# First norm's load order, split last products, and two rests moved from Pool to DVE in a two-layer hybrid trunk

## The reference

```python
def rmsnorm(x, w):
    y = xf * lax.rsqrt(jnp.mean(xf * xf, axis=-1, keepdims=True) + EPS) * w

def attn_pool_mixer(u, w_in, sinks, pool_w, pool_scale, w_out):
    proj = u @ w_in
    ...                                   # a: attention, m: pooled means times pool_w
    return jnp.concatenate([a, m], axis=-1) @ w_out

def swiglu(h, w_gate, w_up, w_down):
    return (jax.nn.silu(h @ w_gate) * (h @ w_up)) @ w_down

    for layer in range(DEPTH):
        h = rmsnorm(x, mix_norm_w[layer])
        x = x + (attn_pool_mixer if layer % 2 == 0 else ssd_mixer)(h, ...)
        x = x + swiglu(rmsnorm(x, ffn_norm_w[layer]), w_gate[layer], w_up[layer], w_down[layer])
    return rmsnorm(x, final_norm_w)
```

## Time and profile before

| | us |
|---|---|
| median of 3 runs | 2375.91 |
| range of the runs | 2374.59 to 2376.46 |
| the profiled execution | 2377.45 |
| its span in the trace | 2375.7 |
| PE busy / DVE / ACT / Pool busy | 2310.3 / 1269.2 / 1067.4 / 1207.6 |

### The profile page before, as it was taken

The page is one execution under the profiler, slowest core; times in us unless marked ns, Lnnn a source line. Parts: engine busy times, 40 slices in busy tenths (PEclk is TensorE's granted clock), DMA queues, the critical chain, the costliest instruction groups (busy, mean ns, idle before and its releaser), DMA issues.

```text
span 2375.7 us, 29380 instructions
## 1 busy us (share of the span) xinstructions
PE 2310.3 (97%) x10850; PEld 1882.3 (79%) x10850; DVE 1269.2 (53%) x1662; ACT 1067.4 (45%) x1888; POOL 1207.6 (51%) x852
## 2 busy tenths in 40 slices
PE   7999999999999999999999999999999999999997
PEld 5867778888888888777877887887878888887886
DVE  6447563333336787467257347438762433335776
ACT  4036553333333446375266248238543333333444
POOL 3223287777774654224224214314287777774653
PEclk9999999999999999999999999999999999999999
DMA  5100223323238753121221212122213323227744
GB/s 154 49 27 19 102 65 118 115 85 115 85 111 287 243 151 94 56 81 54 63 71 54 67 41 89 39 59 80 91 61 132 116 84 116 85 98 275 254 148 142
DMA packets 166786, 247.89 MB, mean 104 GB/s; under 512 B 18416, under 2 KB 111484, under 8 KB 164092
## 3 DMA queue, kind: packets, MB, share of 16 engines
q1 hardware_dynamic: 161020, 230.06, 29.7%
q10 hardware_dynamic: 5632, 15.99, 1.7%
HBM read 192.93 MB, written 53.08 MB: 104 GB/s over the span
## 4 chain that ended last, share of the span: by engine, by line
PE 85%; DVE 6%; issue 2%; ACT 2%; POOL 2%; DMA 1%; SPq 0%; DVEq 0%; ACTq 0%; POOLq 0%
PE ps L1383 27%; PE ps L1385 26%; PE ps L1384 26%; PE ps L1854 1%; POOL p_lo L752 1%; PE ps L1406 1%; DVE acc L2463 1%; PE ps L1841 1%; DVE mdec L2502 1%; DMA d_val<-in_w_down 1%; PE ps L1548 1%; DVE yx L2531 1%; POOL p_val L776 1%; PE ps L1846 1%; PE ps L1569 1%
## 5 line engine op out<-in xcount | busy, mean ns | idle before, releaser
L727 POOL TENSOR_TENSOR w_lo<-w_raw,w_hi 128x1024 fp32r<-128x1024 f32 x74 | 181.2, 2453 | 337.2 <-ACT w_hi L898 327.0
L829 POOL TENSOR_TENSOR s_lo<-s_val,s_hi 128x512 fp32r<-128x512 f32 x154 | 233.8, 1520 | 207.9 <-ACT s_hi L1199 207.7
L1383 PE MATMUL ps<-xn_hi,w_hi 128*128 128x512 f32 x800 | 319.5, 399 | 5.0 <-DVE xn_lo L1976 2.5
L2134 DVE TENSOR_TENSOR xres<-ps,xres 128x512 f32<-128x512 f32 x132 | 90.8, 689 | 433.6 <-PE ps L1385 422.5
L1384 PE MATMUL ps<-xn_lo,w_hi 128*128 128x512 f32 x800 | 314.1, 393 | 0.0
L1385 PE MATMUL ps<-xn_hi,w_lo 128*128 128x512 f32 x800 | 313.7, 392 | 0.0
L1383 PE MATMUL ps<-xn_hi,p_hi 128*128 128x512 f32 x704 | 274.5, 390 | 0.8 <-POOL p_lo L752 0.6
L1385 PE MATMUL ps<-xn_hi,p_lo 128*128 128x512 f32 x704 | 273.9, 389 | 0.0
L1384 PE MATMUL ps<-xn_lo,p_hi 128*128 128x512 f32 x704 | 273.9, 389 | 0.0
L752 POOL TENSOR_TENSOR p_lo<-p_val,p_hi 128x512 fp32r<-128x512 f32 x176 | 237.3, 1357 | 36.5 <-ACT p_hi L1018 36.5
L1018 ACT ACTIVATE p_hi<-p_val 128x512 fp32r<-128x512 f32 x176 | 111.2, 632 | 306.8 <-POOL p_val L776 306.8
(11 more groups left out here) (269 smaller groups left out, 5160.0 us busy)
## 6 DMA issues: line engine op xcount, KB each, us to landing
s_val<-hidden SPq DMA_DIRECT2D x154, 256.0 KB, 2.8
hidden<-xres SPq DMA_DIRECT2D x20, 1792.0 KB, 6.6
wv_g<-in_w_gate SPq DMA_DIRECT2D x22, 1024.0 KB, 5.3
wv_u<-in_w_up SPq DMA_DIRECT2D x22, 1024.0 KB, 5.2
w_raw<-in_ssd_w_in SPq DMA_DIRECT2D x40, 512.0 KB, 3.9
d_val<-in_w_down SPq DMA_DIRECT2D x70, 256.0 KB, 4.0
rows_v<-in_w_down SPq DMA_DIRECT2D x64, 256.0 KB, 3.6
mdec<-decay_sums SPq DMA_DIRECT2D x32, 512.0 KB, 3.7
```

The costliest lines, as they stand in the source:

```text
L727: pool.tensor_tensor(w_lo[piece.slot][:, :], raw[piece.raw][:, :], f(w_hi[piece.slot][:, :]), ALU.subtract).then_inc(lo_done, 1)
L829: pool.tensor_tensor(s_lo[i][:, :], s_val[i][:, :], f(s_hi[i][:, :]), ALU.subtract)\
L1383: pe.matmul(dst, l_hi, r_hi, start=first, stop=False, skip_group_check=reopened)
L2134: dve.tensor_tensor(tmp, bank, tmp, ALU.add).then_inc(c_ready, 1)
```

## The change

**First norm.** SP loads tile 0, the norm weight, tiles 1, 2, 3, then piece 0, piece 1 and tiles 4 to 7; ACT issues none. DVE makes tiles 0 to 2, then one rest, piece 0's hi, make(3), and alternates from there. Tiles 2 to 7 now count as tail, and PE runs the first column sums in another sequence: hi-only products of piece 0 first (`column_sums`), the lo blocks after T(5), T(6) and T(7) within piece 1. ACT makes pieces 2 and 3 after its last tile.

**Pooled output.** `pooled_out(0)` waits per block for its own rest (the first three for rest 3) and goes to bank 4.

**FFN.** Pool keeps T3lo(0) alone; T3lo(1) and T3lo(2) go to DVE (L2070 becomes a loop). M4g's rest goes behind that of M6u on Pool. In pair 1 ACT copies M6g out ahead of the hi copy of M5u.

**Tail.** In layer 1 the slices 8 to 10 of M3 run tile by tile; ACT squares the first half of tiles 4 to 7 during M3 (slices 1 and 2, both layers), and the second half at the end; SP stores tile 6 and half of tile 7; the other half of tile 7 is weighted on Pool, scaled and stored by ACT; tiles 4 and 5 are stored from ACT between the squares.

```diff
+        def po_bank(j):
+            return 7 if j else 4
...
-        lo_order = Order([(0, n) for n in ("M1g", "M2g", "M5g", "M1u", "M2u", "M3g", "M6g", "M7g", "M4g",
-                                           "M5u", "M6u", "M3u", "M7u")]
+        lo_order = Order([(0, n) for n in ("M1g", "M2g", "M5g", "M1u", "M2u", "M3g", "M6g", "M7g",
+                                           "M5u", "M6u", "M4g", "M3u", "M7u")]
...
-                               ("T3", 3), ("T4", 0), ("T4", 1), ("T4", 2), ("T4", 3)])
-        comb_pool_order = Order([("T3lo", 0), ("T3lo", 1), ("T3lo", 2)])
+                               ("T3", 1), ("T3", 2), ("T3", 3), ("T4", 0), ("T4", 1), ("T4", 2), ("T4", 3)])
+        comb_pool_order = Order([("T3lo", 0)])
...
+        LAST = 3
         def down_count(layer, j, p, t_=3):
+            if (layer, j) == (1, len(DOWN) - 1) and p >= NP - LAST:
+                return 4 * (layer * SLICES + j * NP + NP - LAST) + t_ * LAST + p - (NP - LAST) + 1
             return 4 * (layer * SLICES + j * NP + p) + t_ + 1
...
                 .then_inc(norm_w_loaded, 16)
+            for tt in range(1, NT // 2):
+                load_x(tt)
             for n, s in enumerate(srcs):
                 load(Piece(n), *s)
-                if n == 0:
-                    load_x(3)
...
+            sp.wait_ge(final_ready, NT - 1)
+            sp.dma_start(out[0, (NT - 2) * P:(NT - 1) * P, :], xres[:, NT - 2, :]).then_inc(stored, 16)
+            sp.wait_ge(final_ready, NT)
+            sp.dma_start(out[0, (NT - 1) * P:, BANK:], xres[:, NT - 1, BANK:]).then_inc(stored, 16)
...
-                tail_lo3(1)
-                tail_lo3(2)
-                p_lo_of(0, "M4g")
...
                     p_lo_of(p, "M6" + m)
+                    if (p, m) == (0, "u"):
+                        p_lo_of(0, "M4g")
                     p_lo_of(p, "M3" + m)
...
+            pool.wait_ge(half_ready, NT)
+            pool.wait_ge(norm_w_loaded, 16 * 5)
+            pool.tensor_tensor(xres[:, NT - 1, 0:BANK], xres[:, NT - 1, 0:BANK], norm_wp[:, 0:BANK], ALU.mult)\
+                .then_inc(last_weighted, 1)
...
-            for tt in (1, 2):
-                act.dma_start(xres[:, tt, :], x[0, tt * P:(tt + 1) * P, :]).then_inc(x_loaded[tt], 16)
...
+            def half_square(tt, half):
+                act.activation(junk[:, 0:BANK], xres[:, tt, half * BANK:(half + 1) * BANK], ACT.Square,
+                               accum_out=ssq[:, tt:tt + 1]).then_inc(ssq_ready, 1)
+                t.add("tile")
+                act.wait_ge(ssq_ready, t.count("tile"))
+                if half:
+                    act.activation(std[:, tt:tt + 1], ssq[:, tt:tt + 1], ACT.Sqrt, scale=1.0 / DM, bias=std[:, tt:tt + 1])\
+                        .then_inc(std_ready, 1)
+                else:
+                    act.activation(std[:, tt:tt + 1], ssq[:, tt:tt + 1], ACT.Identity, scale=1.0 / DM, bias=eps[:, :])\
+                        .then_inc(half_ready, 1)
...
                 for tt in range(NT):
-                    if tt >= 3:
-                        xhi(tt - 3)
...
                     square(tt, junk[:, :])
-                    if tt in beside:
-                        if beside[tt].n == 2:
-                            act.wait_ge(hi_done, 2)
-                        hi(beside[tt])
-                for tt in range(NT - 3, NT):
-                    xhi(tt)
+                    for c in COPIES_AFTER.get(tt, ()):
+                        xhi(c)
                 t.add("unit", tail)
                 t.add("xhi", NT)
...
+            norm(lambda tt: act.wait_ge(x_loaded[tt], 16), tail=2)
+            act.wait_ge(hi_done, 2)
+            for n in range(2, LEAD):
+                hi(Piece(n))
...
+                    if p == 1:
+                        copy_out(p, "M6g")
                     p_hi_of(p, "M5u")
-                    copy_out(p, "M6g")
+                    if p > 1:
+                        copy_out(p, "M6g")
...
+                    if j == 6 and p in (1, 2):
+                        for tt in range(2 * p + 2, 2 * p + 4):
+                            act.wait_ge(down_added, add_order.count(layer, "M2", tt - 4, 4, 0))
+                            half_square(tt, 0)
...
             def last_square(layer, tt):
+                act.wait_ge(half_ready, t.count("halfsq", tt - 3 - 4))
                 act.wait_ge(down_added, add_order.count(layer, "M3", tt - 4, 4, 1))
-                square(tt, junk[:, :])
...
                 last_square(1, tt)
-            for tt in range(4, NT):
-                store(tt)
-            act.wait_ge(stored, 16 * NT)
+                if tt >= 6:
+                    store(tt - 2)
+            act.wait_ge(last_weighted, 1)
+            act.wait_ge(rstd_ready, 5 * NT)
+            tail_row = xres[:, NT - 1, 0:BANK]
+            act.activation(tail_row, tail_row, ACT.Copy, scale=rstd[:, NT - 1:NT]).then_inc(last_ready, 1)
+            act.wait_ge(last_ready, 1)
+            act.dma_start(out[0, (NT - 1) * P:, 0:BANK], tail_row).then_inc(stored, 16)
...
+            def column_sums(dst, piece, blocks, lows):
+                p_hi, p_lo = split_of(piece)
+                for k in blocks:
+                    if lows:
+                        pe.matmul(dst, p_hi[:, k, :], xn_lo[:, k, 0:BANK], start=False, stop=k == NK - 1)
+                    else:
+                        pe.matmul(dst, p_hi[:, k, :], xn_hi[:, k, 0:BANK], start=k == 0, stop=False)
+                        pe.matmul(dst, p_lo[:, k, :], xn_hi[:, k, 0:BANK], start=False, stop=False)
...
+                    if ready is not None:
...
-                first_T(tt)
-            firsts = []
-            for k in range(2):
-                pe.wait_ge(lo_done, k + 1)
-                firsts.append(begin_unit())
-                if k == 0:
-                    pe.wait_ge(pair_freed, NT // 2)
-                columns(firsts[k][:, 0, :], Piece(k), 0, range(5))
-                for tt in range(NT // 2 + 2 * k, NT // 2 + 2 * k + 2):
-                    first_T(tt, tail=True)
-                columns(firsts[k][:, 0, :], Piece(k), 0, range(5, NK))
-            pe.wait_ge(tail_split, NT // 2)
+                first_T(tt, tail=tt >= 2)
+            firsts = [begin_unit()]
+            pe.wait_ge(lo_done, 1)
+            pe.wait_ge(xn_hi_done, NT // 2)
+            column_sums(firsts[0][:, 0, :], Piece(0), range(4), False)
+            first_T(4, tail=True)
+            column_sums(firsts[0][:, 0, :], Piece(0), range(4, NK), False)
+            first_T(5, tail=True)
+            pe.wait_ge(pair_freed, 2)
+            pe.wait_ge(tail_split, 2)
+            column_sums(firsts[0][:, 0, :], Piece(0), range(NK), True)
+            pe.wait_ge(lo_done, 2)
...
-                rows(ps[:, 7, :], j, pooled).then_inc(po_full, 1)
+                rows(ps[:, po_bank(j), :], j, pooled, ready=None if j else pool_split).then_inc(po_full, 1)
...
-            pe.wait_ge(pool_split, 4)
...
-                            pe.wait_ge(comb_pool_done, comb_pool_order.count(layer, "T3lo", 2))
+                            pe.wait_ge(comb_pool_done, comb_pool_order.count(layer, "T3lo", 0))
...
-                def down_slice(j, p):
+                def down_slice(j, p, tiles=range(4)):
                     s = j * NP + p
                     i = place(s)
-                    pe.wait_ge(s_lo_done, layer * SLICES + s + 1)
-                    pe.wait_ge(d_lo_done, layer * SLICES + s + 1)
-                    for t_ in range(4):
+                    if 0 in tiles:
+                        pe.wait_ge(s_lo_done, layer * SLICES + s + 1)
+                        pe.wait_ge(d_lo_done, layer * SLICES + s + 1)
+                    for t_ in tiles:
...
+                    if layer and s >= SLICES - LAST:
+                        continue
...
+                if layer:
+                    for t_ in range(4):
+                        for p in range(NP - LAST, NP):
+                            down_slice(len(DOWN) - 1, p, (t_,))
...
-                for tt in range(NT):
-                    if tt >= 3:
-                        lo(tt - 3)
-                    if tt >= 1:
-                        make(tt - 1)
-                    if tt in (2, 3):
-                        hi(Piece(tt - 2))
-                lo(NT - 3)
-                make(NT - 1)
-                for tt in range(NT - 2, NT):
-                    lo(tt)
+                for tt in range(3):
+                    make(tt)
+                lo(0)
+                hi(Piece(0))
+                make(3)
+                lo(1)
+                hi(Piece(1))
+                lo(2)
+                lo(3)
+                make(4)
+                for tt in range(5, NT):
+                    make(tt)
+                    lo(tt - 1)
...
-                tail_lo3(3)
+                for i in range(1, 4):
+                    tail_lo3(i)
...
-                    normed(4, tt, xres[:, tt, :], norm_wp).then_inc(final_ready, 1)
+                    if tt == NT - 1:
```

(5 more changed lines are left out.)

30 lines of the change are left out of this document (21 added, 9 removed).

## The result

| | us |
|---|---|
| changed kernel, median of 4 runs | 2359.22 (2358.17 to 2359.52) |
| before, beside it, median of 4 runs | 2375.25 (2372.67 to 2376.46) |
| ratio | 0.9933, 95% interval 0.9918 to 0.9947 |
| profiled execution, span | 2358.17, 2356.4 |

The change saves 16.0 us, 0.7%. The forecast was 2354.5 in a range of 2350.5 to 2362.5, from a sum of 22.1. The time lies in the range, 4.7 above the forecast. Most of what follows is about where the missing 5 to 6 us are.

What follows compares the result with a forecast made beforehand. PE was taken to bound the kernel, leaving only its idle time and half-speed stretches to gain. Terms 3.6 + 3.3 + 11.4 + 3.8 = 22.1 gave 2353.8 us from the median; 2354.5 was taken, range 2350.5 to 2362.5.

Steps and rivals of the forecast that it cites:

- A: First norm: earlier loads and new order start dense work at 19.7, 4.6 earlier; 3.6 us gained, bounds 1 and 5.8.
- B: Pooled output: shorter wait gains 1.66 us, and the slow stretch behind it goes, 1.6 to 1.7 more; together 3.3.
- C: FFN's first and second pairs, both layers: 4.0 + 5.7 + 3.3 - 1.6 = 11.4 us gained, bounds 8 and 13.
- D: Tail: tile-wise last slices, half squares and spread stores end the span 3.8 us earlier, bounds 2.5 and 5.
- What bounds the kernel: PE is busy 2310.3 of 2375.7 us; gain can only come from its 65 us idle and half-speed stretches.
- C, M6g: FFN pair 0: M6g waits for DVE's last T2 rest, slowed by Pool; gains 4.0 us in layer 0, 5.7 in layer 1.
- C, the new wait: FFN: M4g's later rest delays pair 1's load and the copy M7u needs; costs 0.8 us a layer, 1.6 in all.
- R1: Rival: T3 rests moved to DVE run beside Pool's sums, PE waits at M7g and M7u; 2362 us, chance 0.2.
- R2: Rival: the first norm's loads land no sooner, so its gain falls to 1; 2358 us, chance 0.1.
- R3: Rival: M6g really waits for Pool, so the FFN gain keeps only 1.7; 2365 us, chance 0.04.
- R4: Rival: Pool falls behind in the FFN's pairs, PE waits in each of 20; 2428 us at 1.9 each, chance 0.03.
- the likeliest case: The forecast itself, the whole kernel at 2350.5 to 2359 us, chance 0.61.

Runs made afterwards that it cites:

- e6: Changed kernel with M4g's rest put back behind M7g's on Pool: 2359.5 us, beside 2375.73 for the kernel before.
- e4: The changed kernel run again unaltered: 2353.04 us, beside 2374.76 for the kernel before.
- e11: Changed kernel with the first norm's loads issued as before, keeping the new order of work: 2357.33 us, beside 2375.25 for the kernel before.
- e9: Changed kernel with one DVE swap in pair 0, the sum M4g needs ahead of the first hidden block: 2353.82 us, beside 2375.25 for the kernel before.
- e2: Kernel before with only the FFN edits: 2363.68 us, beside 2374.76 for the kernel before.
- e5: Kernel before with only the pooled output edit: 2373.63 us, beside 2375.73 for the kernel before.
- e12: The changed kernel run once more unaltered, in a later set: 2357.55 us, beside 2375.25 for the kernel before.
- e1: Kernel before with only the first norm's new loads and engine orders: 2371.65 us, beside 2374.76 for the kernel before.
- e3: Kernel before with only the tail edits: 2371.02 us, beside 2374.76 for the kernel before.
- e8: Changed kernel with two instead of three last slices tile by tile (LAST = 2): 2355.2 us, beside 2375.73 for the kernel before.

## Why the prediction held, and what in it was too large

By the stages (means over all profiles with and without a part; layer 1 without e6, whose edit lies there):

| term | forecast | measured |
|---|---|---|
| A, first norm | 3.6 | 3.0 |
| B, pooled output | 3.3 | 3.0 |
| C, layer 0 (M6g 4.0, pair 1 1.65, new wait -0.8) | 4.9 | 2.8 |
| C, layer 1 (5.7, 1.65, -0.8) | 6.5 | 5.2 |
| first slices of the down part | 0 | -1.1 |
| D, tail | 3.8 | 4.0 |
| sum | 22.1 | 16.9 |

The measured terms add up to 16.9, and the pooled medians give 17.1. The first set's 16.0 and e4's 21.7 lie on both sides. The SSD part of e4's profile had no drop of the clock and that of the first had two; that this chance made the medians is argued.

**What bounds the kernel.** Right: each gain came out of a PE wait or a slow stretch.

**A.** The start at 19.7 was measured as 20.0 to 20.8. The prediction names 2.28 as the price of make(3) beside Pool and gives its end as 15.4 to 16.5; its sum goes on from the late end, which has room for the 3.40 that it took. What was off is where DVE began it: 14.28 instead of about 13.1, because tile 1's load landed at 8.00 and not at 6.7, so make(3) ended at 17.68. In the first profile the transposes behind it took 1.09 instead of 1.97, which hid most of that. Against it, the distance from the dense start to the small transposes grew by 0.7 on average (means over the eight profiles with the order and loads of part A and the four without), where the forecast took 1.05 off. So 4.6 less 1.0 came out as 3.7 less 0.7. The bound for loads as before (22.3) was met by e11 to 0.2. The half speed at the start came again, as forecast: in the changed kernel's first profile at a granted clock of 0.50, in the earlier trace rows and in e9 at one that reads 1.00.

**B.** Right in both halves.

**C, M6g.** The reading against the page's releaser was right, and decisive: M6g waited for DVE's T2 rest, which waited for Pool's instructions (e2). What was too large was the layer 0 term: 1.8 of its 4.0 was the drop of the clock in one profiled execution. Three others with the same wait have no drop, so a fair price was a quarter of it; by the stages (53.2 against 52.2) the drop cost 1.0 on the whole, since the waits behind it became shorter. In layer 1 the drop was there in all four, 6.8 long in three and 3.4 in e5. The sum's closing sentence named these stretches as its least sure part, but the sum took them at full.

**C, the new wait.** The wait at M7u was forecast with its mechanism and size (0.8 against 0.81). What was missed: DVE's T4 rests can run beside Pool's work too, and PE now comes to M4g earlier. In the kernels with part C they take 2.48 or about 6.06, and where they take 6.06 M4g waits 1.14 to 1.19, unless the sum stands first as in e9. The changed kernel's first profile shows the one in layer 0 and the other in layer 1, e4 and e12 the long form in both. In layer 0 of e1, e5 and e3 three of the four are long as well, and M4g, which PE reaches over 2 us later there, has no wait. What decides between the two forms was not tested. R1 was right in kind (DVE's work contending with Pool, one new wait a layer) and wrong in the place and in the fall of the clock: of the moved T3 rests one at most takes 1.8, and M7g keeps its 0.78. By the rule of the Trainium skill (SBUF — State Buffer, Who interferes with whom), which lets the second of the two engines to start wait in full, the 3.40 of make(3) agrees: it is 2.35 and a little over 1.

**The first slices** were in no step: 1.1 us, with loads that mostly land later, cause open.

**D.** Right in mechanism and size; the 0.97 for `d_lo` was 0.84, and by e8 it lies beside DVE's queue.

**R2** put A at 1 if the loads do not land sooner; e11 makes it 1.9. **R3** is refuted by e2. **R4**: Pool's rests have the same mean as before, and layer 0's pairs 2 to 10 take 346.4 us in all fourteen profiles.

**The numbers.** The range held the time; the likeliest case's own end, 2359, was missed by 0.2.

## What to carry to other kernels

Where a wait ends, ask what the named engine did before: the last instruction to be issued for it may have been held by a third engine, and the duration of its instructions beside and without the other shows it (0.68 against 1.78 here). Where two engines slow each other, moving work from one to the other pays if it leaves them working one after the other; so look also at what both will run in the ten microseconds that follow. A clock that drops behind a wait in one profile is to be priced by how often it drops in several.

## What the runs showed of the hardware that I had not expected

Behind the same wait of about 2 to 2.6 us the granted clock drops to 0.50 for 3.4 us in some executions and not in others of the same program; over the five such waits of the SSD part the count ran from none to five, and the length from 746.2 to 754.4. Behind the wait of 2.62 at the pooled output it dropped in every profile, behind the one of 1.03 in none. And a DVE instruction with two SBUF inputs that starts 30 ns behind a Pool one of 2.35 ends 1.1 after it: 3.40 for 1.28.
